# Moving the loads of cached keys and values from GpSimd's queue to ScalarE's in a one-core hybrid encoder step

## What is computed

```python
xn = rms_norm(x, norm1_g)
aq, ak, av, mq, mk, mv, mi, mf, mo = split_in(xn @ w_in)      # w_in 2048 x 6152
# group 1, attention of each running stream b over 256 cached and 16 new keys
k_all = concat([cache_k[b], k_new]); v_all = concat([cache_v[b], av])
s = q . k_all * scale + bias;  p = softmax(s);  w = p[0] - lam * p[1]
att = rms_norm(w @ v_all, subln_g)
# group 2, an mLSTM with a matrix memory per stream
x = x + concat([att, mlstm]) @ w_out
x = x + square(relu(rms_norm(x, norm2_g) @ w_up)) @ w_down    # 2048 -> 8192 -> 2048
```

## Time and profile before

| | |
|---|---|
| median of 3 runs | 1936.47 us (1936.12 to 1936.97) |
| the profiled execution | 1937.73 us |
| its span, first to last instruction | 1935.9 us |
| mean granted TensorE clock | 0.982 of full speed |
| busy: TensorE, its weight load, VectorE, ScalarE, GpSimd | 97%, 93%, 47%, 36%, 8% |
| bytes from HBM, to HBM | 235.61 MB, 18.84 MB |

### The profile page before, as it was taken

The page is one execution under the profiler, slowest core; times in us unless marked ns, Lnnn a source line. Parts: engine busy times, 40 slices in busy tenths (PEclk is TensorE's granted clock), DMA queues, the critical chain, the costliest instruction groups (busy, mean ns, idle before and its releaser), DMA issues.

```text
span 1935.9 us, 30743 instructions
## 1 busy us (share of the span) xinstructions
PE 1878.5 (97%) x10738; PEld 1807.7 (93%) x10738; DVE 913.6 (47%) x1697; ACT 697.8 (36%) x1317; POOL 152.5 (8%) x197
## 2 busy tenths in 40 slices
PE   6999999999999999999999999999999999999998
PEld 5899988888887888999999999999999999999998
DVE  3443665444445555654443345433444433454332
ACT  5222553444433333543333333333333333333332
POOL 2020000000011101211100011100011000011000
PEclk9999999999997889999999999999999999999999
DMA  8374335663373543434444444444444444444442
GB/s 215 95 216 119 104 92 169 205 215 105 94 213 98 153 142 95 125 109 119 128 122 124 125 122 127 120 129 119 129 120 127 122 123 126 122 128 120 138 140 80
DMA packets 424189, 255.32 MB, mean 132 GB/s; under 512 B 11532, under 2 KB 414272, under 8 KB 424128
## 3 DMA queue, kind: packets, MB, share of 16 engines
q1 hardware_dynamic: 407232, 214.46, 39.6%
q0 software_dynamic: 11248, 38.39, 6.0%
q10 hardware_dynamic: 5648, 1.65, 0.4%
HBM read 235.61 MB, written 18.84 MB: 131 GB/s over the span
## 4 chain that ended last, share of the span: by engine, by line
PE 69%; DVE 1%; ACT 0%; issue 0%; POOL 0%; ACTq 0%; POOLq 0%; DVEq 0%
PE acc L469 21%; PE acc L468 21%; PE acc L470 21%; PE bank L1567 4%; PE bank L1574 1%; PE ssb L495 0%; PE bank L1724 0%; DVE C_rows L1422 0%; DVE a_lo L1454 0%; DVE w_lo L443 0%; ACT w_hi L434 0%; PE ssb L1567 0%; POOL out L533 0%; DVE mvo L1482 0%; POOL n_y L663 0%
## 5 line engine op out<-in xcount | busy, mean ns | idle before, releaser
L443 DVE TENSOR_TENSOR w_lo<-raw,w_hi 128x512 fp32r<-128x512 f32 x768 | 556.2, 731 | 853.6 <-ACT w_hi L434 852.5
L434 ACT ACTIVATE w_hi<-raw 128x512 fp32r<-128x512 f32 x768 | 482.8, 630 | 889.2 <-PE acc L470 872.7
L468 PE MATMUL acc<-a_hi,w_hi 128*128 128x384 f32 (+1 forms) x2048 | 716.0, 350 | 2.4 <-DVE zt L1354 2.4
L469 PE MATMUL acc<-a_lo,w_hi 128*128 128x384 f32 (+1 forms) x2048 | 703.2, 343 | 0.0
L470 PE MATMUL acc<-a_hi,w_lo 128*128 128x384 f32 (+1 forms) x2048 | 698.8, 341 | 0.0
L468 PEld LDWEIGHTS acc<-a_hi,w_hi 128*128 128x128 f32 x2048 | 387.7, 189 | 8.9 <-DVE w_lo L443 3.3
L469 PEld LDWEIGHTS acc<-a_lo,w_hi 128*128 128x128 f32 x2048 | 388.1, 189 | 3.5 <-issue 1.0
L470 PEld LDWEIGHTS acc<-a_hi,w_lo 128*128 128x128 f32 x2048 | 389.2, 190 | 0.0
L469 PE MATMUL acc<-x2g_lo,w_hi 128*128 128x384 f32 x1024 | 348.7, 341 | 0.0
L468 PE MATMUL acc<-x2g_hi,w_hi 128*128 128x384 f32 x1024 | 346.9, 339 | 0.0
L470 PE MATMUL acc<-x2g_hi,w_lo 128*128 128x384 f32 x1024 | 345.3, 337 | 0.0
(11 more groups left out here) (262 smaller groups left out, 989.9 us busy)
## 6 DMA issues: line engine op xcount, KB each, us to landing
raw<-in_w_up SPq DMA_DIRECT2D x128, 512.0 KB, 4.0
raw<-in_w_down SPq DMA_DIRECT2D x128, 512.0 KB, 3.8
raw<-in_w_in SPq DMA_DIRECT2D x96, 512.0 KB, 4.1
raw<-in_w_out SPq DMA_DIRECT2D x32, 512.0 KB, 4.0
kc<-in_cache_k POOLq DMA_DIRECT2D x8, 1024.0 KB, 6.6
vc<-in_cache_v POOLq DMA_DIRECT2D x8, 1024.0 KB, 8.2
C_rows<-in_state_C POOLq DMA_DIRECT2D x8, 512.0 KB, 6.2
out<-C_rows POOLq DMA_DIRECT2D x8, 512.0 KB, 4.5
```

The lines of the kernel that those rows point to most:

```text
L434: e.activation(w_hi[:, q], raw[:, slot, 4 * (q % 2):4 * (q % 2) + 4, :], ACT.Copy).then_inc(hi_ready, 1)
L443: e.tensor_tensor(w_lo[:, q], raw[:, slot, 4 * (q % 2):4 * (q % 2) + 4, :], w_hi[:, q].bitcast(F32), ALU.subtract).then_inc(lo_ready, 1)
L468: e.matmul(out, w_hi[:, q, kk], hi[:, k, at], start=start, stop=False, skip_group_check=True)
L469: e.matmul(out, w_hi[:, q, kk], lo[:, k, at], start=False, stop=False, skip_group_check=True)
```

## The change

The loads of keys for streams 1 to 7 (7 DMAs) and of values for streams 2 to 7 (6 DMAs) are issued by ScalarE. Values of stream n + 2 are issued behind the `osum` step of stream n, keys of stream n + 1 behind the second part of the keys of stream n. The loop on GpSimd goes. The early loads, which stay on GpSimd, get semaphores of their own (`kc_first`, `vc_first0`, `vc_first1`).

```diff
@@ gpsimd
-            dma(kc[:], cache_k[0, 0].rearrange("(a p) h n -> p a (h n)", p=P), "kc_in")
+            dma(kc[:], cache_k[0, 0].rearrange("(a p) h n -> p a (h n)", p=P), "kc_first")
...
-                dma(vc[:, b], cache_v[0, b].rearrange("(a p) h n -> p a (h n)", p=P), f"vc_in{b}")
+                dma(vc[:, b], cache_v[0, b].rearrange("(a p) h n -> p a (h n)", p=P), f"vc_first{b}")
...
-            for b in range(1, BD):
-                done(e, ("kT", b - 1, 3))
-                dma(kc[:], cache_k[0, b].rearrange("(a p) h n -> p a (h n)", p=P), "kc_in")
-                if b >= 2:
-                    done(e, ("o", b - 2))
-                    dma(vc[:, b % 2], cache_v[0, b].rearrange("(a p) h n -> p a (h n)", p=P), f"vc_in{b % 2}")
-
@@ scalar, keys
+                        if n[1] == 1 and n[0] + 1 < BD:
+
+                            done(e, ("kT", n[0], 3))
+                            e.dma_start(kc[:], cache_k[0, n[0] + 1].rearrange("(a p) h n -> p a (h n)",
+                                                                             p=P)).then_inc(S("kc_in"), 16)
@@ scalar, osum
+                        if n + 2 < BD:
+
+                            e.dma_start(vc[:, n % 2], cache_v[0, n + 2].rearrange("(a p) h n -> p a (h n)",
+                                                                                 p=P)).then_inc(S(f"vc_in{n % 2}"), 16)
@@ tensor, out
-                    e.wait_ge(S(f"vc_in{b % 2}"), 16 * (b // 2 + 1))
+                    if b < 2:
+                        e.wait_ge(S(f"vc_first{b}"), 16)
+                    else:
+                        e.wait_ge(S(f"vc_in{b % 2}"), 16 * (b // 2))
@@ tensor, keys
-                        e.wait_ge(S("kc_in"), 16 * (b + 1))
+                        if b == 0:
+                            e.wait_ge(S("kc_first"), 16)
+                        else:
+                            e.wait_ge(S("kc_in"), 16 * b)
```

More of the change, by code:

```diff
@@ L853, in att_work @@
                         if n == 0:
-                            e.wait_ge(S("kc_in"), 16)
+                            e.wait_ge(S("kc_first"), 16)
                         else:
```

## The result

| | runs | median us | ratio to before, 95% interval |
|---|---|---|---|
| before | 18 | 1935.01 | |
| changed | 17 | 1943.5 | 1.0049 (1.0035 to 1.0063) |
| changed, a second time on another occasion (f3 below) | 8 | 1943.75 | 1.0062 (1.0039 to 1.0084) |

One more run of the changed kernel took 3662.33 us at a granted clock of 0.990, for a reason that nothing here shows, and is left out of the table.

The account below looks back on a forecast made before the run. TensorE, busy for 97% of the span, was taken to bound the kernel. Streams 2 to 7 (+6.0), stream 1 (+0.5) and clock (+1.7) gave +8.2 us on 1936.47 us: 1944.7 us, range 1940.5 to 1952.

Parts of the forecast that it names:

- TensorE would wait at all seven streams: Sign of being right: TensorE waits for keys at every stream, about 13 us in all instead of 6.4 us.
- The order decides: Streams 2 to 7: values now go ahead of keys on the same queue, where keys went first; together +1.0 us each.
- The three terms for streams 2 to 7: Landing of keys: megabyte in front, sooner first issue, quicker start; together +1.0 us on each of six streams, +6.0 us.
- A megabyte in front: Streams 2 to 7: keys land behind a megabyte of values on their queue, +2.6 us a stream.
- The first issue sooner: Streams 2 to 7: ScalarE issues values after osum, before GpSimd's old issue, -0.8 us; from below, 0.5 us sooner still.
- A quicker start: Streams 2 to 7: ScalarE's hardware queue, taken to be like SyncE's, starts filling sooner than GpSimd's, -0.8 us a stream.
- Stream 1: Keys without values: issue 1.7 us later, 0.8 us back by quicker start, backlog may swallow it; +0.5 us.
- The clock, one more drop: TensorE's clock falls after long waits at streams 1 and 5; a third drop, expected at stream 3, costs +1.7 us.
- What was costed at nothing: ScalarE's 13 issues (4.8 to 6.4 us) and new kT(b, 3) wait, and GpSimd's 9.1 us of removed issues: worth nothing.
- Faster, the software queue made keys late: Rival: the hardware queue gets both loads through before keys alone used to land; 9.8 us less, 1926.7 us, chance 0.20.
- No change: Rival: early issue and quick start leave +0.3 us a stream, clock stays; under 3.9 us, about 1937.5 us, chance 0.17.
- Much slower, sharing with the raw weights: Rival: ScalarE's queue shares with raw loads, 1.6 us on six streams, five more clock drops; 1961 us, chance 0.10.

Follow-up runs that it names:

- e1: The changed kernel with keys of a stream issued ahead of its values, all on ScalarE's queue; 1930.56 us, ratio 0.9988 to the kernel before.
- f4: The changed kernel with keys issued ahead of values on ScalarE's queue, run again side by side with others; 1934.77 us, ratio 0.9996 to before.
- e2: The kernel before with values of a stream issued ahead of its keys on GpSimd; 1943.89 us, ratio 1.0064 to before.
- e3: Against the changed kernel, keys issued from ScalarE and values from GpSimd, on two queues; 1943.21 us, ratio 1.0063 to before.
- e8: Against the changed kernel, keys issued from GpSimd and values from ScalarE, on two queues; one run, 1950.79 us.
- e5: The changed kernel with keys loaded from ScalarE in two halves of 512 KB, each when its half buffer is free; 1924.7 us against 1934.71 us, ratio 0.9949.
- halves from ScalarE: The changed kernel with each load of keys split into two halves of 512 KB; 1924.7 us, and 1923.01 us when run again.
- halves from GpSimd: The kernel before with each load of keys split into the same two halves; 1930.28 us, and 1930.94 us when run again.

## Why the prediction was right

**TensorE would wait at all seven streams, about 13 us in all.** It does, 13.6 us. That the keys had no slack was the basis of the sum, and it held within 0.3 us: streams 2, 4 and 6 had no wait before and have 1.76, 0.94 and 1.51 us now.

**The order decides.** Shown from both sides: e1 and f4 take the cost away by turning the order back on ScalarE, e2 brings it about on GpSimd.

**The three terms for streams 2 to 7.** Sum forecast +1.0 us each. From TensorE's last read of the buffer to landing, measured now against before, it is +2.0, +0.9, +1.1, +0.5, +1.7 and +1.4 us, 7.8 us together for 6.0 forecast. The size of the single terms was off:
- *A megabyte in front, +2.6 us.* The keys land 3.2 us after the values at stream 2, 2.6 and 2.7 us at 4 and 6, and 3.0 to 3.1 us at 3, 5 and 7.
- *The first issue sooner, -0.8 us.* It was 1.25 us sooner (0.95 us before the last read, instead of 0.30 us after), because the issue doesn't wait for the square to finish. That was the end named from below.
- *A quicker start, -0.8 us.* At streams 2, 4 and 6 there is none: the values, first on ScalarE's queue, take 5.4, 5.2 and 5.7 us to landing, where the keys, first on GpSimd's, took 5.3, 5.4 and 5.4 us. With the keys first, e1 shows 4.80, 5.05 and 5.58 us, where GpSimd's took 5.25, 5.41 and 5.44 us: 0.2 us less on average, 0.45 us at most. This term was too large. The 0.4 us between the two paths that the Trainium skill states (DMA: Bandwidth & Descriptors, section Latency and other measured facts) is nearer to these runs than the rows that were preferred. Those compared the engines' busy share, and a share says little while packets are slow: in the kernel before, the microsecond after 343 has 33 packets of GpSimd's queue at a share of 84.4%, the next one 99 at 103.2%. At streams 3, 5 and 7, where raw weights are moving too, the first load lands 0.8, 1.3 and 0.3 us sooner than before.

At the even streams the three come to 1.6 us instead of 1.0, at the others to 1.0 us. That the sum of six stood as near as it did is in part luck: at the even streams an issue that came sooner than forecast made up for about half of the start that didn't come.

**Stream 1, +0.5 us.** Measured +0.04 us in the wait and +0.2 us in f3, though the issue comes 1.2 us later after the last read than before: the backlog swallowed it, as the term said; the value was on the safe side.

**The clock, one more drop.** In the attention stretch of the profiled execution there are three drops instead of two on the running streams, 5.1 us lost instead of 3.4 us. Stream 3, which was to get the third, has none, and stream 7 has one (stretches after these two waits):

```profile
366.00:370.00 4.00, 3.21 (x21) 3.21 (x22) 2.38 (x6) 0.60 (x1) 0.00 (x0) 1.00 0.38 100
...
440.00:445.00 5.00, 3.91 (x17) 3.90 (x18) 2.60 (x7) 0.75 (x2) 0.00 (x0) 0.66 0.48 129
```

That the count came out is luck: f3, the same kernel, has the same waits and a single drop, at stream 5. After its wait of 2.66 us at stream 1 the clock stays up, and after that of 2.66 us at stream 5 it falls:

```profile
327.00:331.00 4.00, 3.29 (x21) 3.29 (x22) 0.69 (x1) 0.60 (x1) 0.00 (x0) 1.00 0.63 169
...
401.00:405.00 4.00, 2.94 (x12) 2.93 (x13) 1.74 (x5) 0.60 (x1) 0.00 (x0) 0.58 0.39 110
```

With seven waits each, the profiled executions of e2, e3 and e8 have four, one and five drops; e1 and f4, one kernel, have none and one. So neither the length of a wait nor their number tells how many drops an execution has. Over many runs the changed kernel loses 2.1 us more than before, uncertain by 1.9 us, which the forecast 1.7 us fits. That this comes from the waits isn't shown: f4, without the waits at streams 2, 4 and 6, loses 30.3 us beside the 31.1 us of f3.

**What was costed at nothing.** ScalarE's issues and its new wait, and GpSimd's: right. The sign of being wrong was a wait for the split weights, and the one such row of TensorE's in the whole span is not longer than before (total, times, longest; the changed kernel, and 3.3, 3, 2.7 in the kernel before):

```profile
PEld acc L468 <- DVE w_lo L443: 2.7, 3, 2.0
```

Even 20 issues in e5 brought no such wait to the attention stretch.

**The rivals.** *Faster, the software queue made keys late:* its point was that the second load would land before the first used to. No stream reached it; the nearest was stream 5, 0.5 us later than before. But its cause has a true part: on streams 3, 5 and 7 raw weights are in play, and there the first load landed sooner. *No change:* out, both intervals lie above 1. *Much slower, sharing with the raw weights:* sharing does occur, at those streams. The raw load issued at 357.65 us, together with the values, took 9.3 us, and from 361 to 362 us both queues have as many packets (q1 is SyncE's):

```profile
q10 hardware_dynamic: 87, 0.36, 89.0%
q1 hardware_dynamic: 88, 0.05, 15.3%
```

This is the turn by turn of the Trainium skill (same page, section Queues, rings and completion order). It didn't cost the 1.6 us that the rival put on each stream: the packets of some 512 bytes took 15.3% of the engines' time beside 89.0% for as many of 4 KB. And at the even streams, where the raw load comes when the other queue is already moving, it had no packet for nearly two microseconds after its issue at 344.16 us, which the rule doesn't give (packets of 344 to 346 us, and the raw load's time to landing):

```profile
q10 hardware_dynamic: 192, 0.76, 95.4%
raw<-in_w_in SPq DMA_DIRECT2D x1, 512.0 KB, 5.5
```

So the row against the rule, read on GpSimd's queue, holds for ScalarE's at the even streams as well.

## What to carry to other kernels

When loads move to another queue, compare the order in which they stand there before the queue itself: here one swap of two issues is worth 9 to 11 us on either queue (f3 against f4, e2 against the kernel before). The queue is worth little: with keys first, ScalarE's is 2.0 us better in the rest, and with values first there is nothing between the two. A load that lands just in time shows no wait in the profile; compare landing with first use, stream by stream, before anything is put in front of it. And where a single buffer leaves too little room, see whether a part of it is free sooner: halves from ScalarE gave a median of 10 us under the kernel before, which no choice of queue or order did.

## What the runs showed of the hardware that was not expected

- An issue from ScalarE that waits for nothing starts together with the activation in front of it (339.54 and 339.53 us).
- Two queues with a megabyte each didn't share the DMA engines at stream 2 of e3: q0 alone from 341 to 342 us, q10 with 98.6% from 343 to 344 us. At stream 3 of the same run, with the same 0.73 us between the issues, they shared evenly (49 and 52 packets from 361 to 362 us). What sets which of the two happens is open; at stream 3 a raw load was issued 0.3 us ahead of the first.
- The loss by the clock over the whole run differs between two kernels in the same way on two occasions: 26.3 and 26.4 us a run with halves from ScalarE, 28.8 and 31.3 us with halves from GpSimd, 3.7 us together with an uncertainty of 2.3 us. It is open why, and where in the run.
